# Rearranging the per-chunk work of an RWKV-7 mixer inside a two-block transformer kernel

## The reference, cut to what matters

```
z = rmsnorm(h) @ w_in              # 13 groups of 512 columns: lora, k, r, v, conv
log_w = -c * sigmoid(w0 + tanh(wd) @ w_decay_up);  a = sigmoid(a0 + ad @ a_up)
g = sigmoid(gd) @ g_up
kk = k * k_k;  kk = kk / max(sqrt(sum_head(kk * kk)), 1e-12)      # key length
k = k * (1 + (a - 1) * k_a)
y = rwkv7_scan(r, exp(log_w), k, v, -kk, kk * a)                  # over the tokens
y = (y - mean_head(y)) * rsqrt(var_head(y) + eps) * ln_x_w + ln_x_b
y = (y + sum_head(r * k * r_k) * v) * g                           # bonus, gate
mix = concat(y_conv, y) @ w_out
```

## Time and profile before

| | |
|---|---|
| median of 3 runs | 2488.97 us |
| the profiled execution | 2487.17 us, its span 2485.3 us |
| TensorE (PE) matmul busy | 2384.5 us, 96% |
| VectorE (DVE), ScalarE (ACT), GpSimd (POOL) busy | 61%, 41%, 7% |
| granted TensorE clock, mean | 0.985 of 2.4 GHz |

### The profile page before, as it was taken

How to read it: one execution, slowest core, us unless ns; L and a number is a source line. 1 busy time by engine, 2 the same in 40 slices (tenths; PEclk the granted TensorE clock), 3 DMA queues, 4 the chain that set the end, 5 groups by cost and what they waited for, 6 DMA issues and landing times.

```text
span 2485.3 us, 52106 instructions
## 1 busy us (share of the span) xinstructions
PE 2384.5 (96%) x20928; PEld 2270.4 (91%) x20928; DVE 1515.3 (61%) x1891; ACT 1031.3 (41%) x1278; POOL 167.3 (7%) x197
## 2 busy tenths in 40 slices
PE   7998999989899999999999899998999999999996
PEld 7988999989899999999888799887999999998885
DVE  6567465664776656666444566646777677674444
ACT  5442232233544344444444445645444443444442
POOL 2000000000500000000000220004000000000001
PEclk9999999999999999999999999999999999999998
DMA  7534333315465566556666473354556556656663
GB/s 238 160 110 132 95 100 95 104 67 182 139 193 184 179 185 182 180 185 183 189 187 187 140 257 116 119 175 128 188 184 187 185 183 187 186 178 189 189 189 94
DMA packets 116216, 405.91 MB, mean 163 GB/s; under 512 B 12624, under 2 KB 19760, under 8 KB 115824
## 3 DMA queue, kind: packets, MB, share of 16 engines
q1 hardware_dynamic: 109248, 392.22, 51.4%
q10 hardware_dynamic: 6832, 11.68, 1.3%
HBM read 401.69 MB, written 2.15 MB: 162 GB/s over the span
## 4 chain that ended last, share of the span: by engine, by line
PE 87%; issue 6%; DVE 4%; ACT 1%; POOL 0%; ACTq 0%; POOLq 0%; DVEq 0%
PE ps L1560 17%; PE ps L1561 17%; PE ps L1562 17%; PE ps L1556 15%; PE ps L1558 7%; PE ps L1690 3%; PE ps L1679 2%; PE ps L1681 2%; PE ps L1680 2%; PE ps L1892 1%; PE ps L1894 1%; PE ps L1893 1%; DVE wl L881 1%; ACT wh L528 1%; PE ps L1907 1%
## 5 line engine op out<-in xcount | busy, mean ns | idle before, releaser
L881 DVE TENSOR_TENSOR wl<-raw,wh 128x1024 fp32r<-128x1024 f32 x744 | 915.1, 1240 | 784.4 <-ACT wh L528 783.9
L528 ACT ACTIVATE wh<-raw 128x1024 fp32r<-128x1024 f32 x744 | 780.4, 1057 | 1042.6 <-PE ps L1562 572.7
L1560 PE MATMUL ps<-xh,wh 128*128 128x256 f32 (+2 forms) x3456 | 982.5, 284 | 41.7 <-DVE xl L906 32.1
L1561 PE MATMUL ps<-xl,wh 128*128 128x256 f32 (+2 forms) x3456 | 979.9, 284 | 0.0
L1562 PE MATMUL ps<-xh,wl 128*128 128x256 f32 (+2 forms) x3456 | 979.1, 283 | 0.0
L1560 PEld LDWEIGHTS ps<-xh,wh 128*128 128x128 f32 x3456 | 656.5, 190 | 44.4 <-issue 27.8
L1561 PEld LDWEIGHTS ps<-xl,wh 128*128 128x128 f32 x3456 | 657.6, 190 | 0.2
L1562 PEld LDWEIGHTS ps<-xh,wl 128*128 128x128 f32 x3456 | 655.8, 190 | 0.0
L1556 PE MATMUL ps<-act,wh 128*128 128x512 f32 x1408 | 493.1, 393 | 1.6 <-DVE wl L881 1.6
L1558 PE MATMUL ps<-act,wl 128*128 128x256 f32 x1408 | 392.9, 279 | 0.0
L1556 PEld LDWEIGHTS ps<-act,wh 128*128 128x128 f32 x1408 | 263.8, 187 | 64.7 <-DVE wl L881 1.9
(11 more groups left out here) (232 smaller groups left out, 2282.0 us busy)
## 6 DMA issues: line engine op xcount, KB each, us to landing
raw<-in_gate_up SPq DMA_DIRECT2D x176, 512.0 KB, 3.7
raw<-in_down SPq DMA_DIRECT2D x176, 512.0 KB, 4.0
raw<-in_up SPq DMA_DIRECT2D x176, 512.0 KB, 3.7
raw<-in_w_in SPq DMA_DIRECT2D x104, 512.0 KB, 3.7
raw<-in_in SPq DMA_DIRECT2D x48, 512.0 KB, 4.2
raw<-in_w_out SPq DMA_DIRECT2D x32, 512.0 KB, 4.0
raw<-in_out SPq DMA_DIRECT2D x32, 512.0 KB, 3.6
bias<-bias_rows ACTq DMA_DIRECT2D x1, 4096.0 KB, 26.8
```

The source lines that it names most:

```text
L528: act.activation(wh[:, slot], raw[:, slot], ACT.Copy).then_inc(high_ready, 1)
L881: dve.tensor_tensor(wl[:, slot], raw[:, slot], wh[:, slot].bitcast(F32), ALU.subtract).then_inc(low_ready, 1)
L1560: pe.matmul(out, w_high, hi, start=(k == 0), stop=False)
L1561: pe.matmul(out, w_high, lo, start=False, stop=False)
```

## The change

- `piece` cuts groups 2, 3 and 4 into 2, 3 and 3 weight chunks. The halves of the rate's, the decay's and the key lengths' products come after the second and the fifth weight chunk of groups 2, 3 and 4, both in the banks of the group before. ScalarE's list follows the same pattern, its semaphore counts once for each half.
- Maximum, reciprocal, scaling of the keys are cut by token chunk (and the first two by halves of the heads). Chunk 0's stand between the splits of group 5; those of chunks 1 and 2 in chunk 0 and those of chunks 3 and 4 in chunk 1, at levels 1 and 2 and at levels 4 and 5.
- Centering, squares, root, reciprocal and scaling of y, and the bonus, are done for chunk c-1 within chunk c, on 64 tokens. Chunk 4 does its own bonus beside chunk 3's, and its own norm in `center` and `var`. They work in place in `kn` and `z`; `bonus`, `rkr2` and `yc2` go.
- The numbers of half weight chunks by slot are new: 22 in chunks 0 to 3, 16 in chunk 4.
- `gup` is loaded at the end of chunk 3.

The diff, cut:

```diff
-HALVES = {"gram": 2, "turn": 3, "P1": 1, "J1": 2, "P2": 1, "J2": 2, "P3": 1, "J3": 2, "P4": 2, "J4": 2, "P5": 1,
+HALVES = {"gram": 2, "turn": 2, "P1": 1, "J1": 2, "P2": 1, "J2": 2, "P3": 1, "J3": 2, "P4": 1, "J4": 2, "P5": 1,
           "J5": 2, "update": 2, "output": 1}
-LAST_HALVES = {"P3": 1, "J3": 1, "update": 1, "output": 1, "center": 2, "var": 2}
+THIRD_HALVES = {**HALVES, "update": 1, "output": 2}
+LAST_HALVES = {"gram": 2, "turn": 2, "P1": 2, "J1": 2, "J3": 2, "update": 2, "output": 1, "center": 1, "var": 2}
 ...
 # ScalarE, groups 2 to 4
+            highs(20, 2)
+            rates(0)
+            highs(22, 3, 2)
+            rates(1)
+            highs(25, 3, 1)
 ...
+                    if l == 2 and c:
+                        squares_of_y(c - 1)
+                    if l == 3 and c:
+                        spread_of_y(c - 1)
+                    if l == 2 and c < LAST:
+                        decays(c + 1)
+                    if c == LAST and l >= 2:
+                        gates(l - 2)
 ...
 # VectorE, group 5
+            inverse_lengths(0, 0)
+            lows(46, 1, 2)
+            inverse_lengths(0, 1)
+            lows(47, 1, 3)
+            unit_keys(0)
+            lows(48, 1)
             decay_sums()
-            lows(46, 2, 2)
-            inverse_lengths()
-            lows(48, 4)
+            lows(49, 3, 1)
 ...
 # VectorE, the loop: slot "turn"
+                if c:
+                    bonus_keys(c - 1)
 # slot P, ahead of the split
+                    if c < 2 and l in (1, 4):
+                        inverse_lengths(2 * c + 1 + l // 4, 0)
+                    if c < 2 and l in (2, 5):
+                        unit_keys(2 * c + 1 + l // 5)
+                    if c and l == 4:
+                        inverse_spread(c - 1, 1)
+                    if c and l == 5:
+                        bonuses(c - 1, 7)
 # slot J, behind the additions to tn and tt
+                    if c < 2 and l in (1, 4):
+                        inverse_lengths(2 * c + 1 + l // 4, 1)
+                    if c and l == 3:
+                        inverse_spread(c - 1, 0)
+                    if 0 < c < LAST and l == 4:
+                        unit_y(c - 1)
 ...
 # TensorE, groups 2 to 4 (3 and 4 in the same pattern)
+            piece(2, 0, 2)
+            pe.wait_ge(group_read, 2)
+            per_tile(4, 0, rate_up, lambda f, k: z[0:LORA, 1, 1:L + 1], L)
+            piece(2, 2, 5)
+            pe.wait_ge(pre_act, 3)
+            per_tile(4, 1, rate_up, lambda f, k: z[0:LORA, 1, 1:L + 1], L)
+            piece(2, 5, 8)
 ...
+            def whole_heads(b, lhs, rhs, c, done):
+                n = CHUNK_LENGTHS[c]
                 for f in range(RT):
+                    last = pe.matmul(ps[:, b, C * f:C * f + n], lhs, rhs(f), start=True, stop=True)
+                last.then_inc(done, 1)
 ...
+                if c and name == "J1":
+                    pe.wait_ge(zb_ready, c + 1)
+                    centers(c - 1)
+                if c and name == "J2":
+                    spreads(c - 1)
+                if c and name == ("J4" if c < LAST else "J3"):
+                    pe.wait_ge(yroot_ready, c)
+                    bonus_sums(c - 1, 7)
+                    if c == LAST:
+                        bonus_sums(c, 5)
+                if c == LAST and name in ("P2", "P3"):
+                    gates(("P2", "P3").index(name))
                 fill(SLOT[c, name])
```

More of the change, by code:

```diff
@@ L655, in _, with rates, decay_rates, lengths @@
             act.activation(z[:, 2:4, 1:L + 1], z[:, 2:4, 1:L + 1], ACT.Sigmoid).then_inc(pre_act, 1)
[L656 to L663, removed]
+            def rates(half):
+                act.wait_ge(pre_pe, 1 + half)
+                for f in range(4 * half, 4 * half + 4):
+                    last = act.activation(b_[:, f], ps[:, 4 + f % 4, 0:L], ACT.Sigmoid, bias=vcol("a0", f))
+                last.then_inc(pre_act, 1)
+            def decay_rates(half):
+                act.wait_ge(pre_pe, 3 + half)
+                for f in range(4 * half, 4 * half + 4):
+                    last = act.activation(sw[:, f], ps[:, f % 4, 0:L], ACT.Sigmoid, bias=vcol("w0", f))
+                last.then_inc(pre_act, 1)
+            def lengths(half):
+                act.wait_ge(pre_pe, 5 + half)
+                act.activation(rkr[:, TILE_HALF[half]], ps[:, 4:8, 0:L], ACT.Sqrt).then_inc(pre_act, 1)
+            highs(20, 2)
[3 more added lines that the diff above has]
+            highs(25, 3, 1)
+            highs(28, 2)
+            decay_rates(0)
+            highs(30, 3, 2)
+            decay_rates(1)
             act.wait_ge(pre_dve, 1)
             act.activation(rkr[:], kn[:], ACT.Square).then_inc(pre_act, 1)
[L666 to L669, removed]
+            highs(33, 3, 1)
+            highs(36, 2)
+            lengths(0)
+            highs(38, 3, 2)
+            lengths(1)
+            highs(41, 3, 1)
             def decays(c):
@@ L714, in _ @@
                 refill(SLOT[c, "gram"])
[L715 to L718, removed]
+                if c < LAST:
                     act.wait_ge(k_turned, c + 1)
@@ L1137, in conv_rest @@
                                 ALU.mult, ALU.add)
-                        last.then_inc(dve_step, 1)
-                        conv_step[0] = steps.add()
+                        if tap == 2:
+                            last.then_inc(taps_done, 1)
+                        else:
+                            last.then_inc(dve_step, 1)
+                            conv_step[0] = steps.add()
                     elif part == 2 and age == 0:
-                        dve.wait_ge(dve_step, conv_step[0])
+                        dve.wait_ge(taps_done, half + 1)
                         dve.wait_ge(group_read, g + 1)
@@ L1186, in gated_bonus, with bonus_keys @@
[L1186 to L1190, removed]
+            def bonus_keys(c):
+                now = slice(1 + T0[c], 1 + T0[c] + CHUNK_LENGTHS[c])
+                zr = z[:, 12:20, now]
+                r_k = vec[:, VEC["r_k"]:VEC["r_k"] + RT].unsqueeze(2).broadcast_to([P, RT, CHUNK_LENGTHS[c]])
+                dve.tensor_tensor(zr, zr, r_k, ALU.mult).then_inc(dve_step, 1)
+                dve.wait_ge(dve_step, steps.add())
+                dve.tensor_tensor(zr, zr, z[:, 4:12, now], ALU.mult).then_inc(bonus_keys_ready, 1)
@@ new lines, in bonuses, with inverse_spread @@
+            def bonuses(c, b):
+                n, now = CHUNK_LENGTHS[c], slice(1 + T0[c], 1 + T0[c] + CHUNK_LENGTHS[c])
+                dve.wait_ge(bonus_done, c + 1)
+                dve.tensor_tensor(z[:, 20:28, now], z[:, 20:28, now], bank(b)[:, :, 0:n], ALU.mult).then_inc(bonus_ready, 1)
+            def inverse_spread(c, half):
+                part = ysq[c][:, TILE_HALF[half], 0:CHUNK_LENGTHS[c]]
+                dve.wait_ge(yroot_ready, c + 1)
+                dve.reciprocal(part, part).then_inc(dve_step, 1)
+                steps.add()
@@ new lines, in unit_y, with gated_bonus @@
+            def unit_y(c):
+                n, t0 = CHUNK_LENGTHS[c], T0[c]
+                dve.wait_ge(dve_step, steps.n)
+                dve.tensor_tensor(kn[:, :, t0:t0 + n], kn[:, :, t0:t0 + n], ysq[c][:, :, 0:n], ALU.mult).then_inc(yn_ready, 1)
+            def gated_bonus(t0, t1, landed_bonuses):
+                dve.wait_ge(pre_act, 11)
+                dve.wait_ge(bonus_ready, landed_bonuses)
+                for f in range(RT):
+                    last = dve.scalar_tensor_tensor(z[:, 20 + f, 1 + t0:1 + t1], z[:, 20 + f, 1 + t0:1 + t1], vcol("ln_b", f),
+                                                    gate[:, f, t0 - TG:t1 - TG], ALU.add, ALU.mult)
@@ L1704, in join @@
                 heads(6, [(lambda f: qb[:, f], lambda f: tt[:, f])], dt_done)
-            def centers(b, width, tiles, t0, t1):
+            def whole_heads(b, lhs, rhs, c, done):
+                n = CHUNK_LENGTHS[c]
                 for f in range(RT):
-                    last = pe.matmul(ps[:, b + f // tiles, width * (f % tiles):width * (f % tiles) + t1 - t0], center[:],
-                                     kn[:, f, t0:t1], start=True, stop=True)
-                last.then_inc(pre_pe, 1)
@@ L1712, in spreads @@
-            def spreads(b, width, tiles, t0, t1):
-                for f in range(RT):
-                    last = pe.matmul(ps[:, b + f // tiles, width * (f % tiles):width * (f % tiles) + t1 - t0], bones[:],
-                                     yc2[:, f, t0:t1], start=True, stop=True)
-                last.then_inc(pre_pe, 1)
-            def extra(name):
-                if name == "gram":
-                    pe.wait_ge(pre_dve, 7)
-                    pe.wait_ge(group_read, 13)
-                    per_tile(0, 0, lambda f, k: bones[:], lambda f, k: rkr2[:, f, :], LG)
-                elif name == "turn":
-                    pe.wait_ge(bonus_ready, 1)
-                    per_tile(0, 1, lambda f, k: bones[:], lambda f, k: rkr2[:, f, :], LG)
-                elif name == "P1":
```

(25 more changed lines are left out.)

228 lines of the change are left out of this document (101 added, 127 removed).

## The result

| | before | after |
|---|---|---|
| median | 2489.28 us (2488.17 to 2490.11, 4 runs) | 2473.08 us (2468.52 to 2474.39, 4 runs) |
| ratio | | 0.9934, 95% interval 0.9922 to 0.9946 |
| profiled execution, its span | 2487.17, 2485.3 us | 2472.43, 2470.6 us |

What follows compares the result with a forecast made beforehand. TensorE, busy 96% of the span, was taken as the bound. Removed 32.0 us, added matmuls 13.0 and new waits 3.0 gave -16.0: span 2469.3, median 2473.0 us, 0.64% faster, range 2464 to 2484.

Steps and rivals of the forecast that it cites:

- Weight groups, products in the middle (-5.5 and -3.4): Weight groups: three waits of 1.8 us on VectorE's read go, -5.5; the clock fall after the second goes, -3.4.
- Weight groups, the reciprocal (-8.9 and -1.7): Group 5: TensorE's 8.9 us stand behind the 13.75 us key-length reciprocal goes, and 1.7 us lost to slow clock.
- The ledger of group 5: VectorE's work in group 5, summed until split 49 at 25.2; TensorE wants that chunk at 27, 1.8 us to spare.
- Chunk 4 (-9.4 and -3.1): Chunk 4: waits of 9.4 us from whole-length VectorE work go, and 3.1 us lost to slow clock.
- granted clock 1.00 from 40 to 570 us: Sign of a right forecast: TensorE's granted clock stays at 1.00 from 40 to 570 us.
- The added matmuls (+13.0): TensorE: 15 center, spread and bonus groups at 1.85 us, 27.8 against 14.8 before, +13.0; +17 or +33 as higher estimates.
- is a weight load's: Narrow center, spread and bonus groups: a floor of 0.116 us a record, not columns, sets the time; weight loads cause it.
- New waits (+3.2 less 0.5): Chunks 0, 1 and 4: four new TensorE waits of 1.5, 0.5, 0.6, 0.6, less 0.5: +2.7, called 3.
- VectorE late in the loop: Rival: VectorE late by 2 us in each of chunks 0 to 3, +8, 2481; chance 0.15.
- Floor and columns one after the other: Rival: narrow groups' floor runs before the columns, 2.5 us a group of 64 columns, +8, 2481; chance 0.08.
- Stops that bring down the clock in each chunk: Rival: stops of about 1.5 us in all five chunks, each followed by slow clock, 24.5 on top, 2497; chance 0.06.
- Weight chunk 49 or 50 missed: Rival: VectorE misses that weight chunk (3 + 3.4) and is late in the loop too, 2487 to 2488; chance 0.07.

Runs made afterwards that it cites:

- e1: Changed kernel with the halves of the rate's, decay's and key lengths' products between the weight groups again: 2481.33 us, ratio 0.9976 to the kernel before.
- e5: Changed kernel with products between the weight groups and key lengths whole again, leaving norm, bonus, gate and new half-chunk numbers: 2489.23 us, ratio 1.0006.
- e2: Changed kernel with maximum, reciprocal and scaling of all key lengths as whole instructions in weight group 5 again: 2481.22 us, ratio 0.9976.
- e8: The changed kernel measured again, with no edit: 2469.51 us, ratio 0.9929 to the kernel before.
- e4: Changed kernel with center, spread and bonus sums in 64 x 64 blocks, not the 128 x 128 matrix: 2459.42 us, ratio 0.9887.
- e7: e4 with the second half of chunk 2's key lengths moved from behind chunk 0's level 4 additions to behind weight group 7's read: 2457.33 us, ratio 0.9876.
- e3: Kernel before with only the weight-group changes (products in the middle of groups, key lengths by token chunk): 2468.44 us, ratio 0.9923.
- e6: Changed kernel with two half reciprocals together, ahead of the additions (key lengths at levels 1 and 4, norm at level 3): 2476.36 us, ratio 0.9945.

## Why the prediction was right, point by point

- **Weight groups, products in the middle (-5.5 and -3.4).** Right: no wait on z is left, and e1 brings back 5.5 us of them and 8.3 us of time. The clock's -3.4 is what one execution happened to show, not a fixed price: 6.8 us at half rate before, 3.4 in e1, 10.2 in e5.
- **Weight groups, the reciprocal (-8.9 and -1.7).** Right: e2 brings back both. It costs 8.1 us where 10.6 less the 0.6 that chunk 0 gets back were expected; the rest is within the spread of the medians (11.7 from e8's). The ledger of group 5 can be laid beside VectorE's timeline in the changed kernel:

```profile
164.60 1.75 DVE L1045 RECIPROCAL rkr<-rkr 128x256 f32<-128x256 f32 x1
166.27 1.16 DVE L891 TENSOR_TENSOR wl<-raw,wh 128x1024 fp32r<-128x1024 f32 x1
167.35 0.68 DVE L1053 SCALAR_TENSOR_TENSOR kn<-kn,rkr 128x512 f32<-128x512 f32 x1
...
170.45 4.39 DVE L1034 TENSOR_TENSOR_SCAN cum<-reset,sw 128x272 f32<-128x272 f32 x7
174.76 3.47 DVE L891 TENSOR_TENSOR wl<-raw,wh 128x1024 fp32r<-128x1024 f32 x3
```

  A half reciprocal takes 1.75 (1.74 worked out), a scaling 0.68 (0.7), and from the read of group 4 (start 154.12) to the end of the scans (174.84) it is 20.7 us; the ledger has 24.0 - 2.5 = 21.5.
- **Chunk 4 (-9.4 and -3.1).** The waits went, the clock only in part. The changed kernel shows 0.98 over its last stretch, (1 - 0.98) x 75.8 / 0.5 = 3 us at half rate, 1.5 lost that I had at nothing; the sign "granted clock 1.00 from 40 to 570 us" was missed there. In e8 it was met: clock 1.00, and chunk 4 is 1.5 us shorter (74.26).
- **The added matmuls (+13.0), the largest doubtful term.** Right in size, with one sign missed: 1.85 us or less had been named for these rows, and at 64 columns they show 2.00 us busy. What the path pays is the time from start to next start, 1.81 us; for 16 columns it is 1.70 (the row at 543.21 in the earlier trace rows, up to the next matmul below), so 48 more columns cost 0.11.

```profile
544.91 0.36 PE L1679 MATMUL ps<-ych,wh 128*128 128x258 f32 x1
```

  By this measure the groups before took 14.2 us and take 12 x 1.81 + 3 x 1.70 = 26.8 now, +12.6. Over chunks 1 to 3 the nine groups less three lost pairs of halves make +7.2 in the stretches; I had 9 x 1.85 - 3 x 3.2 = 7.1. That columns do not set this time is shown, by 1.70 against 1.81 and by e4. That the floor "is a weight load's", as the prediction says, is argued and not shown: e4 fits it, but there the two blocks also run side by side.
  The rule of the Trainium skill against which I set this (TensorE: Matmul & The Clock Gate, What overlaps and what doesn't) gave 2.6 us a group as an estimate. The 1.81 us here say no. From rows alone, floor and columns one after the other would be 16 x (1.70/16 - 0.013 + 0.053) = 2.3 us; and a single load's record lasts 0.19 us here while one starts every 0.113. So on full 128 rows too, one matmul's weight load runs beside another's columns. The formula of the Trainium skill for a load's time (same page, LDWEIGHTS) gives 107 ns for 128 columns. That is near the pace of these groups, 1.81/16 = 0.113 us, and not near the 0.19 us of a load's record.
- **New waits (+3.2 less 0.5).** Mis-sized: four places expected with 1.5, 0.5, 0.6 and 0.6; found 0.9, 0.3, none and 0.3, so 1.5 less the 0.5. The cause of the largest was right (e2, e7). Each was high by 0.2 to 0.6; which entry of the ledger made it so was not traced.
- **The sum.** Too many waits (1.7 us) and too little slow clock (1.5) cancel, and that the medians meet within 0.1 us is luck: the same kernel measured again gave 2469.51. The span came out 1.3 us above the one forecast: the weight groups won 0.7 less, the loop lost 0.3 less than the sum had, and 0.9 is lost behind chunk 4. Norm, bonus and waits in the loop were forecast at -12.5 + 13.0 + 2.7 = +3.2; the stretches show -1.9 + 7.2 - 2.1 = +3.2, of which 1.5 is the fall of the clock that e8 lacks. The times of e3 and e5 are compatible with it.
- **Rivals.** VectorE late in the loop: no wait on tn or tt and 21.7 us idle in chunk 1, and e6 shows what it takes. Floor and columns one after the other: no, 1.81 and not 2.5. Stops that bring down the clock in each chunk: no chunk from 0 to 3 shows a clock under 1.00, not even where e6 puts stops of up to 1.6. Weight chunk 49 or 50 missed: no wait on wl before 560 us.

## What to carry to other kernels

When one engine is busy 96% of the time, price what a rearrangement adds to that engine before counting the waits it removes: here 9.4 us of waits and 3 us of slow clock were bought with 13 us of matmuls. Narrow matmuls against a full-width constant matrix cost nearly the same for 16 columns as for 64 (1.70 and 1.81 us for eight); if the matrix is block diagonal, issue the blocks (1.03). And a long instruction on the engine that feeds the bound one is best cut where its result is used, which took 2 us at a time from a stretch with room and gave back a stop of 8.9.

## What the runs showed of the hardware

In the changed kernel the clock fell once in chunk 4, between 516 and 520 us, with no stop of TensorE over 0.35 us in that chunk before it. What the engine did before: the gate's products, a product of the recurrence, and two bonus groups back to back, 32 records in 3.75 us with few columns for each load of weights. First the matmuls, then the stretch with its clock, both of the changed kernel, and the stretch of the same work when it ran again (e8):

```profile
512.22 3.75 PE L1763 MATMUL ps<-z,bones 128*128 128x64 f32 x32
```

```profile
510.00:523.00 13.00, 13.00 (x139) 12.31 (x138) 6.91 (x8) 4.13 (x7) 0.00 (x0) 0.87 0.00 1
```

```profile
508.00:524.00 16.00, 16.00 (x212) 15.01 (x211) 10.06 (x16) 5.29 (x9) 0.00 (x0) 1.00 0.10 34
```

The same instructions, 0.87 in one execution and 1.00 in another. Of the other traces with the whole groups, e1, e5 and e6 show a fall as well that sets in while the two bonus groups run or right behind them, and e2 shows none; the nine groups in chunks 1 to 3 are followed by none anywhere. With blocks, e4 shows no fall in chunk 4, and e7 shows one 10 us behind its bonus blocks (0.72 from 512 to 518 us), with TensorE busy all the while. So a busy TensorE is no guarantee of its clock, the narrow groups are not proven to be the cause, and what decides between the two stays open.
